# Hybrid decoder trunk: value projections and output products interleaved singly with attention, weight low halves on VectorE

## What is computed

```
x = x + 0.5 * swiglu(rms_norm(x), ...)
h = rms_norm(x);  P = h @ W_in, split into columns
A: sparse attention, 6 heads x 64: an indexer scores all keys, the best 128 are kept,
   logits get a bias by distance, softmax, values
B: gated DeltaNet, 6 heads x 64: causal convolution (width 4), silu, norms,
   chunks of 64: a triangular inverse, then a recurrence over 8 chunks, output norm, gate
C: attention into 256 memory tokens, 4 heads x 64
x = x + concat(A, B, C) @ W_out
x = x + 0.5 * swiglu(rms_norm(x), ...)
```

## Time and profile before

| what | us |
|---|---|
| median of three runs | 2524.82 |
| lowest and highest | 2522.16, 2528.42 |
| the profiled execution | 2525.76 |
| its span, first to last instruction | 2522.9 |

### The profile page before, as it was taken

The page is one execution under the profiler, slowest core; times in us unless marked ns, Lnnn a source line. Parts: engine busy times, 40 slices in busy tenths (PEclk is TensorE's granted clock), DMA queues, the critical chain, the costliest instruction groups (busy, mean ns, idle before and its releaser), DMA issues.

```text
span 2522.9 us, 33880 instructions
## 1 busy us (share of the span) xinstructions
PE 2405.3 (95%) x14076; PEld 1900.6 (75%) x14076; DVE 1086.3 (43%) x1488; ACT 762.8 (30%) x1009; POOL 501.9 (20%) x352
## 2 busy tenths in 40 slices
PE   6999999799999999999999999998999999999999
PEld 5888887577766678888878888865777666788887
DVE  4334335857523243433343333358584232433322
ACT  3222224544322232222232222235443222322221
POOL 4111012264202141110111111122641121311100
PEclk9999999899756699999999999998997557999999
DMA  3222222121200023222222222221211000222222
GB/s 148 100 100 89 96 99 101 51 85 36 77 1 17 3 82 100 100 98 92 94 86 98 100 96 92 94 86 67 68 52 60 1 17 30 71 99 100 96 92 79
DMA packets 28331, 192.31 MB, mean 76 GB/s; under 512 B 3136, under 2 KB 3264, under 8 KB 9536
## 3 DMA queue, kind: packets, MB, share of 16 engines
q1 hardware_dynamic: 27936, 189.80, 22.1%
q10 hardware_dynamic: 288, 0.94, 0.1%
HBM read 188.64 MB, written 2.10 MB: 76 GB/s over the span
## 4 chain that ended last, share of the span: by engine, by line
PE 86%; DVE 7%; ACT 3%; POOL 3%; issue 1%; DMA 0%; DVEq 0%; SPq 0%; POOLq 0%; ACTq 0%
PE psum L830 23%; PE psum L831 23%; PE psum L832 23%; PE psum L1212 4%; PE psum L1224 3%; PE psum L1196 2%; POOL sg L620 1%; ACT wh L1280 1%; POOL sg L624 1%; DVE acc L1672 1%; PE psum L1088 1%; PE psum L948 1%; PE psum L1103 1%; DVE wl L1597 1%; PE psum L1134 1%
## 5 line engine op out<-in xcount | busy, mean ns | idle before, releaser
L830 PE MATMUL psum<-XH,wh 128*128 128x512 f32 x1920 | 780.3, 406 | 25.8 <-DVE XL L1579 14.6
L831 PE MATMUL psum<-XL,wh 128*128 128x512 f32 x1920 | 757.6, 395 | 0.0
L832 PE MATMUL psum<-XH,wl 128*128 128x512 f32 x1920 | 756.3, 394 | 0.0
L830 PEld LDWEIGHTS psum<-XH,wh 128*128 128x128 f32 x1920 | 366.2, 191 | 128.0 <-issue 31.4
L831 PEld LDWEIGHTS psum<-XL,wh 128*128 128x128 f32 x1920 | 366.3, 191 | 81.7 <-issue 7.4
L832 PEld LDWEIGHTS psum<-XH,wl 128*128 128x128 f32 x1920 | 365.0, 190 | 80.3
L1280 ACT ACTIVATE wh<-raw 128x2048 fp32r<-128x2048 f32 x86 | 164.6, 1914 | 488.2 <-PE psum L832 488.2
L1597 DVE TENSOR_TENSOR wl<-raw,wh 128x2048 fp32r<-128x2048 f32 (+1 forms) x86 | 155.9, 1813 | 350.2 <-ACT wh L1280 350.1
L830 PE MATMUL psum<-HH,wh 128*128 128x512 f32 x704 | 278.1, 395 | 0.0
L832 PE MATMUL psum<-HH,wl 128*128 128x512 f32 x704 | 278.1, 395 | 0.0
L831 PE MATMUL psum<-HL,wh 128*128 128x512 f32 x704 | 278.1, 395 | 0.0
(11 more groups left out here) (242 smaller groups left out, 2486.1 us busy)
## 6 DMA issues: line engine op xcount, KB each, us to landing
raw<-weights SPq DMA_DIRECT2D x144, 1024.0 KB, 5.0
raw<-weights SPq DMA_DIRECT2D x32, 896.0 KB, 4.7
xT<-xt SPq DMA_DIRECT2D x4, 512.0 KB, 9.7
memT<-memt SPq DMA_DIRECT2D x2, 1024.0 KB, 4.9
out<-xT SPq DMA_DIRECT2D x8, 256.0 KB, 6.0
stripsA<-strip_table SPq DMA_DIRECT2D x2, 768.0 KB, 4.5
stripsB<-strip_table SPq DMA_DIRECT2D x2, 768.0 KB, 7.4
cst<-masks ACTq DMA_DIRECT2D x1, 833.5 KB, 8.7
```

The costliest lines, as they stand in the source:

```text
L830: pe.matmul(out_ap, a_hi, b_hi, start=first, stop=False)
L831: pe.matmul(out_ap, a_hi, b_lo, start=False, stop=False)
L832: return pe.matmul(out_ap, a_lo, b_hi, start=False, stop=last)
```

## The change

- Low halves: POOL's part (`split_rest`) and its semaphore go; DVE makes the whole low half of every unit, in the same `ev` step.
- The value groups `va` and `vb` leave the fill of the inversion. Each of the slots 0 to 15 is followed by four k-steps of them (12 matmuls), and every second slot by the evacuation. They use PSUM bank 5, so each group waits until the one before is evacuated. The fill is paced over what is left, the last group in it being the last key group, whose norm follows just ahead of `ready`.
- The recurrence keeps to bank 4 for both chunks; the second half of `u` becomes a step of its own, ahead of the second chunk.
- The memory output of slots 4 to 19 goes into `mqT`, over the memory queries that are no longer needed, instead of into `XH`. A new step `msplit` behind slot 19 waits until all values are projected and makes both halves of it at once (ACT a copy and DVE a subtraction of 128x1024). The first job of the next phase waits for ACT's copy alone.
- The output products `op` follow singly behind slots 21 to 28, in bank 5, each waiting until DVE has added the one before.

The diff, cut to its core:

```diff
+FIRST_V = GROUP_AT["va", 0]
+GROUP_BANK = [5 if i >= FIRST_V else i % 2 for i in range(N_GROUPS)]
...
-RECURRENCE = [("u",)]
+RECURRENCE = [("u", 0)]
 for _b in range(NB):
-    RECURRENCE += [("r1", _b, 0), ("r2", _b, 0), ("r1", _b, 1)]
+    RECURRENCE += [("r1", _b, 0), ("r2", _b, 0)] + [("u", 1)] * (_b == 0) + [("r1", _b, 1)]
     if _b:
...
-    for name, c in ([("mq", 1)] + [("dq", c) for c in range(3)] + [("dk", c) for c in range(3)]
-                    + [("va", b) for b in range(NB)] + [("vb", b) for b in range(NB)]):
-        cost = {"va": 0.36, "vb": 0.33}.get(name, 0.68)
-        fill += [(name, c, k, cost) for k in range(KD)]
+    for name, c in [("mq", 1)] + [("dq", c) for c in range(3)] + [("dk", c) for c in range(3)]:
...
-    ops = iter(range(KD))
+    ops = [("op", c) for c in range(KD)]
+    values = [(name, b, k) for name in ("va", "vb") for b in range(NB) for k in range(KD)]
+
+    def piece(n):
+        if n < M_JOBS:
+            for name, b, k in values[:4]:
+                gi = GROUP_AT[name, b]
+                if order[-1][0:2] == ("mm", gi):
+                    order[-1] = ("mm", gi, order[-1][2], k + 1)
+                else:
+                    order.append(("mm", gi, k, k + 1))
+                if k == KD - 1:
+                    order.append(("ev", gi))
+            del values[:4]
+        elif n == M_JOBS + 3:
+            order.append(("msplit",))
+        elif n >= M_JOBS + 5 and ops:
+            order.append(ops.pop(0))
 
     def att(n):
         for _ in range(n):
             n = next(slots, None)
             if n is not None:
                 order.append(("att", n))
-
-    r = 0
+                piece(n)
+
     for step in RECURRENCE:
         order.append(step)
-        if step[0] == "u":
+        if step == ("u", 0):
             att(4)
-        elif step[0] == "r1":
-            att(2)
-            r += 1
-            if r in (5, 6):
-                put(*[("op", next(ops)) for _ in range(KD // 2)])
-        elif step[0] == "r2":
+        elif step[0] in ("r1", "r2"):
             att(2)
...
-                        if U_MIX + 2 <= v - 2 < U_MIX + 18:
-                            sp.wait_ge(S["w_lo_pool"], 16 * L + v - 2 - U_MIX - 1)
...
-                    def split_rest(gi):
-
-                        u = GROUPS[gi]["unit"]
-                        if LAST_OF_UNIT[u] == gi:
-                            slot = u % 2
-                            pool.wait_ge(S["w_hi"], U0 + u + 2 + 1)
-                            pool.tensor_tensor(wl[slot][:, LO_DVE:, :], raw[slot][:, LO_DVE:, :],
-                                               wh[slot][:, LO_DVE:, :].bitcast(F32), ALU.subtract
-                                               ).then_inc(S["w_lo_pool"], 1)
...
                             wait_split(g["unit"])
-                            if gi >= 2:
+                            if gi > FIRST_V:
+                                wait_copied(gi - 1)
+                            elif 2 <= gi < FIRST_V:
                                 wait_copied(gi - 2)
-                        dst, kind = bank[gi % 2], g["kind"]
...
                         if c == 0:
-                            pe.wait_ge(S["o_lo"], NB)
-                        n = SLOT_BEFORE[c]
-                        pe.wait_ge(S["jm_done"], n + 1)
-                        if c >= 2:
-                            pe.wait_ge(S["x_part"], c - 1)
-                        out_rows(0, c, bank[c % 2], True, True).then_inc(S["pr_done"], 1)
+                            pe.wait_ge(S["m_lo"], of("m_lo", 1))
+                            wait_copied(N_GROUPS - 1)
+                        else:
+                            pe.wait_ge(S["x_part"], of("x_part", c))
...
+                            pe.wait_ge(S["x_part"], of("x_part", KD))
...
-                            pe.wait_ge(S["o_lo"], 2 * NB)
+                            pe.wait_ge(S["o_lo"], NB)
...
-                            if j in (0, H_A) and n:
-                                pe.wait_ge(S["o_lo"], phase(n)[2])
+                            if n == M_JOBS:
+                                wait_copied(N_GROUPS - 1)
+                            p = phase(n)[2]
+                            if j in (0, H_A) and 1 <= p <= NB:
+                                pe.wait_ge(S["o_hi"], p)
+                            elif j == 0:
...
-                            act.activation(XH[:, c0:c1, b * P:(b + 1) * P],
+                            dst = XH[:, 0:3, :] if ph else mqT
+                            act.activation(dst[:, :, b * P:(b + 1) * P],
...
+                        elif kind == "msplit":
+                            act.wait_ge(S["o_hi"], NB)
+                            act.wait_ge(S["pj_done"], N_GROUPS)
+                            act.activation(XH[:, 6:8, :], mqT[:, :, :], ACT.Copy).then_inc(S["m_hi"], 1)
...
-                        if 0 <= n < N_JOBS and phase_end(n):
+                        if M_JOBS <= n < N_JOBS and phase_end(n):
...
-                                split_lo(U0 + u + 2, LO_DVE)
+                                split_lo(U0 + u + 2)
...
+                        elif kind == "msplit":
+                            dve.wait_ge(S["m_hi"], of("m_hi", 1))
+                            dve.tensor_tensor(XL[:, 6:8, :], mqT[:, :, :], XH[:, 6:8, :].bitcast(F32), ALU.subtract
+                                              ).then_inc(S["m_lo"], 1)
```

More of the change, by code:

```diff
@@ L308, in _order @@
     put(*[("rd", 3, c) for c in OUT_ORDER])
-    assert not rounds
+    assert not rounds and not ops and not values
     return order
 MIX_ORDER = _order()
-SLOT_BEFORE, OPS_BEFORE = {}, {}
-_slot = _ops = 0
-for _step in MIX_ORDER:
-    if _step[0] == "att":
-        _slot = _step[1]
-        OPS_BEFORE[_slot] = _ops
-    elif _step[0] == "op":
-        SLOT_BEFORE[_step[1]] = _slot
-        _ops += 1
 GDN_COUNTS = dict(eg_ps=3, eg_done=3, tg_done=4, el_done=1, qe_done=1, dt_ps=4, dt_done=4, dm_done=4, kn_ps=4,
@@ L461 @@
 o_ev o_t o_hi o_lo
-pr_done x_part
 """.split()
@@ L1119, in gdn @@
                         elif kind == "u":
[L1120 to L1125 removed]
+                            ch, = at_
+                            if ch == 0:
+                                pe.wait_ge(S["w_done"], of("w_done", NB))
+                                pe.wait_ge(S["v_done"], NB)
+                                pe.wait_ge(S["qe_done"], of("qe_done", 1))
+                                pe.wait_ge(S["sz_done"], of("sz_done", 1))
+                            values(0, ch)
                         elif kind == "r1":
@@ L1133, in gdn @@
                                 for pair in range(3):
-                                    mm = pe.matmul(bank[4 + ch][rows[ch], pair * P:(pair + 1) * P],
+                                    mm = pe.matmul(bank[4][rows[ch], pair * P:(pair + 1) * P],
                                                    WT[:, b, pair, ch * DH:(ch + 1) * DH], Sbd[:, pair, :],
@@ L1170, in values @@
                         for hh, par, pair, h in heads:
-                            mm = pe.matmul(bank[4 + ch][rows[ch], h * DH:(h + 1) * DH], XTF[rows[ch], b, hh, :],
+                            mm = pe.matmul(bank[4][rows[ch], h * DH:(h + 1) * DH], XTF[rows[ch], b, hh, :],
                                            gvN[rows[ch], b, h * DH:(h + 1) * DH], start=(h == 0), stop=(b + ch == 0),
@@ L1716, in evac @@
                         dve.wait_ge(S["pj_done"], gi + 1)
-                        name, c, src = g["name"], g.get("c"), bank[gi % 2]
+                        name, c, src = g["name"], g.get("c"), bank[GROUP_BANK[gi]]
                         if name == "sm":
@@ L1738, in out_part @@
                     def out_part(c):
-                        dve.wait_ge(S["pr_done"], c + 1)
-                        dve.tensor_tensor(xT[:, c, :], bank[c % 2][:, :], xT[:, c, :], ALU.add
+                        dve.wait_ge(S["pr_done"], of("pr_done", c + 1))
+                        dve.tensor_tensor(xT[:, c, :], bank[5][:, :], xT[:, c, :], ALU.add
                                           ).then_inc(S["x_part"], 1)
```

42 lines of the change are left out of this document (16 added, 26 removed).

## The result

The changed kernel took 2539.7 us (median of five runs, 2537.25 to 2540.7), the kernel before 2524.8: 1.0058 times as long, 95% interval 1.0044 to 1.0073. It is slower, by 15 us. The profiled execution has a span of 2535.5 us, 12.6 more than before, and two views show the outline.

The account below looks back on a forecast made before the run. TensorE, busy 95%, was taken as the bound through idle time, work and clock. Per layer the terms summed to -11.5 us if the clock holds, +1.5 if it falls at slot 12; one of each gave 2515, range 2488 to 2545.

Parts of the forecast that it names:

- Part 3: Value pieces in slots 0 to 15: +3 us per layer with full clock from slot 1 or 2 on.
- a fall at slot 12: Clock lost at the wait after slot 11, slots 12 to 15 slower: +13 us, expected in one of two layers.
- Part 2: Values leave the inversion: -5 us in its levels, +2 at its end, sum -3 per layer, bounds -18 and +3.
- Rival A: In slots 0 to 15 the clock never rises: +40 us per layer, 2605 us; chance 10%.
- its milder branch: Rival A with the clock up for the 256-column half of the pieces only: +15 us per layer, 2555 us.
- clock 0.5 in slots 2 to 8: The sign in the trace that was to show Rival A.
- Part 1: Low halves to VectorE in the convolution stretch: held VectorE steps and TensorE waits go, -6.5 us, bounds -9.5 and -2.
- Rival C: In the inversion, GpSimd's mask products and VectorE's wide splits exclude each other: +7 us per layer, 2529 us; chance 10%.
- Part 4: Memory output in place of its queries, copy and subtraction after slot 19: +2 us per layer, bounds 0 and +3.
- Part 5: Output products singly behind slots 21 to 28, bringing back full clock: -7 us per layer, bounds -15 and +12.
- Rival B: The inversion stays bound by TensorE, so the removed work counts nearly whole: -18 us in Part 2, 2485 us; chance 8%.
- Rival D: Pieces find no gaps to fill in slots 0 to 15; already in the sum, gain only in clock and Part 1.

Follow-up runs that it names:

- e10: The edits of e3, e4 and e8 together on the changed kernel: 2468.5 us, 0.9784.
- e6: Kernel before, with VectorE making the whole low half only for the ten mixer units split ahead of the inversion: 2504.7 us, 0.9929.
- e1: Kernel before, with VectorE making the whole low half of every mixer unit and GpSimd none: 2546.2 us, 1.0073.
- e7: Changed kernel, with seven eighths of the low halves of the four units split inside the inversion back on GpSimd: 2510.2 us, 0.9961.
- e8: Changed kernel, with the last key norm's sum moved behind slot 0, its root and product behind slot 1: 2504.9 us, 0.9933.
- e3: Changed kernel, with the second value group's pieces 256 columns wide instead of 128, the added columns zero: 2515.4 us, 0.9966.
- e4: Changed kernel, with the splits of the last two units moved from behind slots 7 and 15 to behind 16 and 17: 2522.8 us, 0.9995.
- e9: Changed kernel, with the value units exchanged, narrow groups in slots 0 to 7 and wide ones in 8 to 15: 2535.8 us, 1.0063.
- e11: The edits of e10 and e7 together on the changed kernel: 2474.1 us, 0.9805.
- e5: The edits of e3 and e4 together on the changed kernel: 2495.1 us, 0.9885.

## Why the prediction was wrong

The forecast was 2515, 10 us faster than the kernel before; the time is 2539.7, 15 us slower, though within the range of 2488 to 2545. The step that failed is a term of Part 3: "I expect full clock from slot 1 or 2 on", and the fall that it allowed "at slot 12". The clock came at slot 3 and went at slot 9, in both layers. Against e10's 59.4 us at 1.00 from slot 0 to slot 16, the change's 84.5 are 4.5 in slots 0 to 3, 8.1 in slots 9 to 11 and 11.9 in slots 12 to 15 (and 0.6 for slot 8's wait).

The prediction had priced two of these: 3 us for the first slots, and 13 for a fall at slot 12, which it put in one of the two layers. What its sum lacked is the fall in the other layer (13), slots 9 to 11 at the lower level (8.1 per layer), and, per layer, 1.5 in slots 0 to 3 and 0.6 at slot 8; that makes 33. Part 2's levels gave back 5.6 per layer more than forecast and the fall at slot 12 cost 1.1 less, 13 in both layers. That leaves 20 of the 24.7 between 2515 and 2539.7; the rest is small terms, and the distance of the medians from the profiled executions. That the time stayed in the range was luck: without the 11 us that the levels gave back beyond the forecast it would be 2551.

Rival A had the right reason (pieces half 128 columns wide, PE covered at 0.50 all the same), and its milder branch is what came, the clock up beside the 256-column half only; it put +15 per layer on that, where +5.5 was measured in layer 0. It stood at 10%. Its sign ("clock 0.5 in slots 2 to 8") would not have shown it, since the fall came at slot 9. The rows did not decide it: the earlier trace rows show narrow pieces at either level, none longer than 5 us, and I took "dense" as one thing for pieces of 128, 256 and 512 columns.

- **Part 1** (predicted -6.5): right in its place, -7.1 in the changed kernel, -5.9 in layer 0 of e6. No convolution step is long any more, and no indexer sum. But the reason was right for one of PE's two large waits only: the indexer's has gone from 5.1 us to 1.4, the one for the squares, 7.9, which was booked as waiting for held DVE steps too, is 8.6 now. From 430 us on, the stretch of 56.3 us takes 49.2; PE idles 3.9 us less, and its matmuls take 3.3 less, at a clock of 0.96 instead of 0.88, which was not in the sum. Below are the two groups of DVE steps, that stretch, and PE's waits from 430 to 541 us:

```profile
L1698 DVE SCALAR_TENSOR_TENSOR gkT<-cv,colsb,gkT x18: 742/752/753, 449.4 to 1720.4; 128x512 f32<-128x512 f32 x18
...
L1667 DVE SCALAR_TENSOR_TENSOR acc<-rl,wI,acc x42: 479/618/754, 426.0 to 1723.7; 128x256 f32<-128x256 f32 x14, 128x384 f32<-128x384 f32 x14, 128x512 f32<-128x512 f32 x14
```

```profile
430.00:479.20 49.20, 39.25 (x177) 28.87 (x175) 42.28 (x72) 22.62 (x41) 0.00 (x0) 0.96 0.19 65
```

```profile
PE psum L935 <- ACT nsq L1343: 8.6, 1, 8.6
PE psum L948 <- ACT rl L1360: 1.6, 2, 1.4
```

  Wrong was to book the wide splits of the inversion at 1.86 us of DVE's spare time: e1 and e7 put 5 to 7 us on the path of layer 0, and in e1 the clock was down behind it besides. Rival C named that price (+7 per layer), but put it on POOL's masks; e1's rows show plain order of work on DVE instead. The rule of the Trainium skill that the prediction named (SBUF — State Buffer, "Who interferes with whom") is borne out where it was used: with GpSimd's subtraction gone, the longest convolution step went from 4.27 to 0.75 us. Where it spoke against the change, it was small: in e7, with GpSimd's subtractions put back, one norm product is held, 1.71 us instead of 0.75, no mask is longer, and the levels are shorter all the same.
- **Part 2** (-5 in the levels, +2 behind them): -10.6 and +2.2. The direction was right. The 99 us for the levels charged 9 for waits and 2 to 3 for clock on top of DVE's work; measured are 94.8 us with DVE busy 82.3 (87%, as the prediction's sign had it), 12.5 idle in all. The +2 was right in time and wrong in what it costs: its two waits also take the clock, 4.5 us more in slots 0 to 3 (e8). Its sign, 4 us or more of waits ahead of slot 0, was 2.52 + 2.23.
- **Part 3** (+3, or +16): +25.2, as above. What was right in it: the wait at slot 12, at full clock 1.22 us where 1.6 was expected, and what its fall costs. "About 1 us shows" behind slot 15 was 2.88 in e3.
- **Part 4** (+2): +2.7. PE's wait for the squares, 1.5 us before, is 3.51 (shown above). No run has this part alone.
- **Part 5** (-7): -7.3 (51.6 to 44.3). The clock is back right behind the first product, at 772.5, and stays until the wait of 2.62 at r1(3, 0), as described. These products have 512 columns, so what they do says nothing of narrow pieces. No run has this part alone either; the gain is read from the stretch.
- **Rival B** (the inversion stays PE-bound, -18) is excluded: PE is busy 78.9 of 94.8 us. **Rival D** was in the sum.

Left open: why the fall comes at slot 9 in the change and at slot 12 in e7 and e8, with a wait of the same 0.6 us at slot 8. Taking away either the wait ahead of slot 0 (e8) or the one at slot 8 (e4) is enough to move it.

## What to carry to other kernels

Work that is moved into a stretch at the lower clock is not fill: before giving it a price, look in the trace for the same matmul shape, among work of the same kind, bringing the clock up and holding it, and take the price at the lower level if no row shows that. Waits of half a microsecond to three, harmless by themselves, are to be removed ahead of such a stretch first; here two small edits of order, e4 and e8, were worth 17 and 35 us, and with wide pieces (e10) 71. And a cost of 1.9 us on an engine that is 76% busy is on the path wherever its next result is what PE waits for; the same edit gained 19 us on the units ahead of the inversion and cost 41 on those inside and behind it.

## What the runs showed of the hardware

- Narrow and wide pieces take nearly the same time at the upper level (slots 9 to 11 take 13.5 us in e8 with narrow ones and in e10 with wide ones, at 0.97 and 1.00), but in the slots they differ in the clock. With narrow ones it did not come up in 51 us of PE covered from end to end (e9), nor from slot 9 to slot 15 (the change); with wide ones it came up behind the first piece (e9) or the third (the change) and stayed to slot 15 over waits of 0.46 and 1.22 us (e3). This is a finding on pieces among attention slots and no law of the width: in the inversion of the kernel before, the clock came back at 664.1, after 10 us at 0.50, among narrow pieces, and in e1, among the same matmuls, it did not. More columns for nothing made the kernel 24 us faster. The added columns hold zeros; that wide pieces without zeros do the same is seen in e9's slots 8 to 15. The Trainium skill, TensorE: Matmul & The Clock Gate, Part 1, has it that "the default state is throttled, and activity releases the throttle". By that alone a PE that the profile shows covered for 51 us should be at 2.4 GHz; e9's trace does not agree, so being busy in the profile and that activity are not the same thing, and no run here tells what counts.
- A wait of 1.22 us in the same place was followed by a fall of the clock among narrow pieces each time (both layers of e4, e7 and e8) and, among wide pieces, in one layer of e11 and in neither of e3, e5 and e10.
